# Down projections of a four-layer network on one core: seven block products in place of eight

## The reference

```python
def second_block(x, c, ...):                     # x: 512 tokens x 1024
    for l in range(DEPTH):                       # DEPTH = 2
        mod = silu(c) @ w_mod[l] + b_mod[l]
        sh1, sc1, gt1, sh2, sc2, gt2 = split(mod, 6)
        h = rms_norm(x, norm_g[l, 0]) * (1.0 + sc1) + sh1
        y = mixer_block(h, ...)                  # four mixers and w_o
        x = x + gt1 * rms_norm(y, norm_g[l, 1])
        h = rms_norm(x, norm_g[l, 2]) * (1.0 + sc2) + sh2
        y = square(relu(h @ w_up[l])) @ w_down[l]    # 1024 -> 4096 -> 1024
        x = x + gt2 * rms_norm(y, norm_g[l, 3])
    return x
```

## Time and profile before

| | |
|---|---|
| time, median of 3 runs | 1938.79 us (1936.28 to 1939.19) |
| span of the profiled execution | 1936.7 us |
| PE busy | 1863.5 us, 96% |
| DVE busy | 1182.6 us, 61% |
| ACT busy | 812.3 us, 42% |
| POOL busy | 79.3 us, 4% |
| chain of waits that ended last | PE 79%, DVE 13%, ACT 3%, issue 2% |
| granted TensorE clock, mean | 0.991 |

### The profile page before, as it was taken

The page is one execution under the profiler, slowest core; times in us unless marked ns, Lnnn a source line. Parts: engine busy times, 40 slices in busy tenths (PEclk is TensorE's granted clock), DMA queues, the critical chain, the costliest instruction groups (busy, mean ns, idle before and its releaser), DMA issues.

```text
span 1936.7 us, 25888 instructions
## 1 busy us (share of the span) xinstructions
PE 1863.5 (96%) x9834; PEld 1476.1 (76%) x9834; DVE 1182.6 (61%) x1991; ACT 812.3 (42%) x1362; POOL 79.3 (4%) x78
## 2 busy tenths in 40 slices
PE   6999998999999999999999999999999999999997
PEld 3777566887566777777988888887777898888886
DVE  5897668886698887656843234335754684323435
ACT  4554543343323345466633234224455654223322
POOL 0002100000201121000000000000000000000000
PEclk9999999999999999999999999999999999999999
DMA  9566035885001553111212222322211212222232
GB/s 368 192 224 239 1 126 204 309 329 209 8 9 39 183 186 109 66 66 66 87 49 105 90 105 87 109 88 104 92 66 44 88 66 80 94 102 93 87 109 87
DMA packets 45533, 230.72 MB, mean 119 GB/s; under 512 B 5017, under 2 KB 7066, under 8 KB 27004
## 3 DMA queue, kind: packets, MB, share of 16 engines
q1 hardware_dynamic: 45436, 229.41, 33.2%
HBM read 227.16 MB, written 2.10 MB: 118 GB/s over the span
## 4 chain that ended last, share of the span: by engine, by line
PE 79%; DVE 13%; ACT 3%; issue 2%; DMA 1%; SPq 0%; POOL 0%; DVEq 0%; ACTq 0%
PE banks L2274 15%; PE banks L2275 15%; PE banks L2276 15%; PE banks L2644 3%; PE banks L2646 3%; PE banks L2645 3%; PE banks L2538 3%; PE banks L2558 2%; PE banks L2459 2%; DVE mod_raw L1410 1%; PE banks L2673 1%; PE banks L2685 1%; PE banks L2699 1%; PE banks L2472 1%; DVE w_low L1395 1%
## 5 line engine op out<-in xcount | busy, mean ns | idle before, releaser
L2274 PE MATMUL banks<-h_high,w_high 128*128 128x512 f32 x888 | 350.0, 394 | 11.4 <-DVE w_low L1395 7.9
L1395 DVE TENSOR_TENSOR w_low<-w_raw,w_high 128x1024 fp32r<-128x1024 f32 x180 | 219.8, 1221 | 230.7 <-ACT w_high L573 230.3
L2275 PE MATMUL banks<-h_low,w_high 128*128 128x512 f32 x888 | 346.6, 390 | 0.0
L2276 PE MATMUL banks<-h_high,w_low 128*128 128x512 f32 x888 | 346.6, 390 | 0.0
L573 ACT ACTIVATE w_high<-w_raw 128x1024 fp32r<-128x1024 f32 x180 | 189.7, 1054 | 151.8 <-PE banks L2276 123.8
L2274 PEld LDWEIGHTS banks<-h_high,w_high 128*128 128x128 f32 x888 | 167.4, 188 | 53.2 <-DVE w_low L1395 12.6
L2276 PEld LDWEIGHTS banks<-h_high,w_low 128*128 128x128 f32 x888 | 167.3, 188 | 35.2
L2275 PEld LDWEIGHTS banks<-h_low,w_high 128*128 128x128 f32 x888 | 167.5, 189 | 34.8 <-issue 0.7
L2276 PE MATMUL banks<-hidden_high,w_low 128*128 128x512 f32 x480 | 186.8, 389 | 0.0
L2275 PE MATMUL banks<-hidden_low,w_high 128*128 128x512 f32 x480 | 186.7, 389 | 0.0
L2274 PE MATMUL banks<-hidden_high,w_high 128*128 128x512 f32 x480 | 186.7, 389 | 0.0
(11 more groups left out here) (543 smaller groups left out, 3459.3 us busy)
## 6 DMA issues: line engine op xcount, KB each, us to landing
w_raw<-in_wt SPq DMA_DIRECT2D x129, 1024.0 KB, 5.0
mod_raw<-in_wmod SPq DMA_DIRECT2D x128, 512.0 KB, 5.1
mod_first<-in_wmod SPq DMA_DIRECT2D x8, 1024.0 KB, 11.5
cmp_w<-in_cmp_w SPq DMA_DIRECT2D x4, 1024.0 KB, 6.9
x<-in_xT SPq DMA_DIRECT2D x2, 1024.0 KB, 7.2
dft<-in_dft SPq DMA_DIRECT2D x2, 1024.0 KB, 8.1
out_x<-x SPq DMA_DIRECT2D x8, 256.0 KB, 2.1
hy_w<-in_hy_w SPq DMA_DIRECT2D x8, 192.0 KB, 3.2
```

Of the source, the lines that this page charges most:

```text
L1395: v.tensor_tensor(low[:, :, :].rearrange("p k c -> p (k c)"), RAW[b // 2][:, b % 2, :], high[:, :, :].rearrange("p k c -> p (k c)").bitcas ...
L2274: mm(out, high[:, k, :], H[:, kk, :], start=start and k == order[0], stop=False)
L2275: mm(out, high[:, k, :], L[:, kk, :], start=False, stop=False)
L2276: last = mm(out, low[:, k, :], H[:, kk, :], start=False, stop=stop and k == order[-1])
```

## The change

The down product is done in four chunks of 1024 hidden features. After each chunk's up tiles (eight; they are no longer followed by a separate round) its product is a 2x2 block product: rows in two halves of 256 tokens, hidden features in two halves of 512, output features in two halves of 512. Eight block products become seven in Winograd's form of Strassen's scheme, with sums and differences of the blocks as operands. A block product is 2 (groups of 128 tokens) x 4 (groups of 128 hidden features) x 3 = 24 matmuls of 128x512. The activations now stand still in the array and the weights move, so y comes out token-major, 128 tokens on the partitions, and is turned by 32 transposes per layer at the end.

PE runs a chunk's seven products as eight steps w = 0 to 7 and a last product. Steps 0 to 3 add the four hidden groups of three products (named by i: 0 into bank A, 1 into E, 2 into D), steps 4 to 7 those of three others (banks A, F, D); each step is 18 matmuls. The seventh product, of 24 matmuls, comes last. Operands of weights stand in two sets, used in turn. What a step needs: one or three column sums of raw weight blocks (POOL), high parts (ACT), low parts (DVE). Between them DVE folds finished banks into the sums of y. The sums of rows of the hidden activations, with their high and low parts, are made by ACT and DVE beside the up tiles.

Core of the diff (functions of PE, POOL, DVE and ACT in this order):

```diff
             for c in range(CHUNKS):
+                for b in range(PER_CHUNK if c else 0):
+                    ...
+                    tile(Q + 8 + 2 * c + b // 4, b % 4, Hh, Hl).then_inc(w_used, 1)
+                for w in range(8):
+                    p, s, late = w % PK, w % 2, w >= PK
+                    for i in ((2, 0, 1) if w in (0, 2, 3, 4, 5, 6) else (0, 2, 1) if w == 7 else (0, 1, 2)):
+                        pe.wait_ge(*when(f"mix_l.{c}.{w}.{2 if late else 'last'}" if i == 2 else f"mix_l.{c}.{w}.0"))
+                        ...
+                        for j in range(2):
+                            if w == PK and i in (0, 2):
+                                pe.wait_ge(*when(f"y2_r.{c}.d{j}" if i == 2 else f"y2_k.0.{j}" if c == 0 else f"y2_r.{c}.a{j}"))
+                            ...
+                            product(out, (high, low), (OPh[s][:, i, :], OPl[s][:, i, :]), start, p == PK - 1).then_inc(*did(f"mix_p.{c}.{w}.{i}.{j}"))
+                for j in range(2):
+                    pe.wait_ge(*when(f"y2_r.{c}.u{j}"))
+                    ...
+                        last = product(bank(BANK_A + j), (S3h[:, p, t], S3l[:, p, t]), (T3h[p][:, :], T3l[p][:, :]), p == 0, p == PK - 1)
+                    last.then_inc(*did(f"mix_v.{c}.{j}"))
-            for n in range(14):
-                tile(Q + 20 + n // 4, n % 4, HIDh, HIDl, even=n % 2 == 0, hidden=1 if n < 2 else None).then_inc(w_used, 1)
...
+            def col_sum(c, w):
+                pool.wait_ge(*when(f"blocks{RAW_OF[w]}.{c}.{w}"))
+                if w >= 2:
+                    pool.wait_ge(*when(f"mix_p.{c}.{w - 2}.2.1"))
+                ...
+                gp.tensor_tensor(OPf[w % 2][:, 2, :], raw[:, 2, :], raw[:, 0, :], sub).then_inc(*did(f"mix_s.{c}.{w}.0"))
+            def late_sums(c, w):
+                ...
+                gp.tensor_tensor(t3[:, :], raw[:, 3, :], raw[:, 2, :], sub).then_inc(*did(f"mix_s.{c}.{w}.0"))
+                pool.wait_ge(*when(f"mix_s.{c}.{w}.0"))
+                pool.wait_ge(*when(f"mix_p.{c}.{w - 2}.0.1"))
+                gp.tensor_tensor(out[:, 0, :], t3[:, :], raw[:, 0, :], add).then_inc(*did(f"mix_s.{c}.{w}.1"))
+                pool.wait_ge(*when(f"mix_s.{c}.{w}.1"))
+                pool.wait_ge(*when(f"mix_p.{c}.{w - 2}.1.1"))
+                gp.tensor_tensor(out[:, 1, :], raw[:, 1, :], out[:, 0, :], sub).then_inc(*did(f"mix_s.{c}.{w}.2"))
...
+            def blocks_low(c, w):
+                dve.wait_ge(*when(f"mix_h.{c}.{w}.0"))
+                v.tensor_tensor(flat(OPl[w % 2], 0, 2), flat(BLOCKS[RAW_OF[w]], 0, 2), flat(OPh[w % 2], 0, 2).bitcast(f32), sub).then_inc(*did(f"mix_l.{c}.{w}.0"))
+            def late_low(c, w):
+                dve.wait_ge(*when(f"mix_h.{c}.{w}.0"))
+                v.tensor_tensor(OPl[w % 2][:, 2, :], BLOCKS[RAW_OF[w]][:, 3, :], OPh[w % 2][:, 2, :].bitcast(f32), sub).then_inc(*did(f"mix_l.{c}.{w}.2"))
+                dve.wait_ge(*when(f"mix_h.{c}.{w}.2"))
+                v.tensor_tensor(flat(OPl[w % 2], 0, 2), flat(OPf[w % 2], 0, 2), flat(OPh[w % 2], 0, 2).bitcast(f32), sub).then_inc(*did(f"mix_l.{c}.{w}.0"))
+                v.tensor_tensor(T3l[w % PK][:, :], T3f[w % PK][:, :], T3h[w % PK][:, :].bitcast(f32), sub).then_inc(*did(f"mix_l.{c}.{w}.last"))
+            def fifth_sum(c, j):
+                gather(c, "d", j, YT[:, j::2, 1, :], twice(BANK_D + j), f"mix_p.{c}.3.2.{j}", ...)
+            for c in range(CHUNKS):
+                ...
+                for w in range(2, PK):
+                    blocks_low(c, w)
+                    sum_low(c, w)
+                for w in range(PK, 8):
+                    late_low(c, w)
+                    if w == 4:
+                        for j in range(2):
+                            fifth_sum(c, j)
+                        for j in range(2):
+                            first_sum(c, j)
+                    if w == 6:
+                        for j in range(2):
+                            second_sum(c, j)
...
+            def late_high(c, w):
+                act.wait_ge(*when(f"blocks{RAW_OF[w]}.{c}.{w}"))
+                act.wait_ge(*when(f"mix_p.{c}.{w - 2}.2.1"))
+                nc.scalar.activation(OPh[w % 2][:, 2, :], BLOCKS[RAW_OF[w]][:, 3, :], ACT.Copy).then_inc(*did(f"mix_h.{c}.{w}.0"))
+                act.wait_ge(*when(f"mix_s.{c}.{w}.0"))
+                nc.scalar.activation(T3h[w % PK][:, :], T3f[w % PK][:, :], ACT.Copy).then_inc(*did(f"mix_h.{c}.{w}.1"))
+                act.wait_ge(*when(f"mix_s.{c}.{w}.2"))
+                nc.scalar.activation(flat(OPh[w % 2], 0, 2), flat(OPf[w % 2], 0, 2), ACT.Copy).then_inc(*did(f"mix_h.{c}.{w}.2"))
```

More of the change, by code:

```diff
@@ L565, in _ @@
+            if lay + 1 < LAYERS:
+                sp.wait_ge(*when(f"mix_l.{CHUNKS - 1}.6.last"))
+                load_pair(first + PER_LAYER // 4, 0)
+        for m in range(NT):
+            sp.wait_ge(*when(f"y2_x.{m}"))
+            sp.dma_start(A["out"][:, m * P:(m + 1) * P].rearrange("(k p) t -> p k t", p=P), XT[:, :, m * P:(m + 1) * P]).then_inc(*did(f"stored.{m}", 16))
+        sp.wait_ge(*when(f"stored.{NT - 1}"))
     @block.scalar
@@ new lines, in totals @@
+            def totals(j):
+                one, six = SUM1[j], SUM6[j][:, :]
+                pool.wait_ge(*when(f"y2_r.{CHUNKS - 2}.v{j}"))
+                gp.tensor_tensor(six, six, one, add).then_inc(*did(f"y2_p.{j}"))
+                gp.tensor_tensor(YT[:, j, 0, :], YT[:, j, 0, :], one, add).then_inc(*did(f"y2_q.{j}"))
+                pool.wait_ge(*when(f"y2_p.{j}"))
+                gp.tensor_tensor(YT[:, j, 1, :], YT[:, j, 1, :], six, add).then_inc(*did(f"y2_c.{j}"))
+                for h in range(2):
+                    gp.tensor_tensor(YT[:, 2 + j, h, :], YT[:, 2 + j, h, :], six, add).then_inc(*did(f"y2_d.{j}.{h}"))
@@ L1387, in _ @@
+            for m in range(2):
+                pool.wait_ge(*when(f"y2_t.{m}"))
+                gp.tensor_tensor(XT[:, :, m * P:(m + 1) * P], XT[:, :, m * P:(m + 1) * P], YF[:, m, :, :], add).then_inc(*did(f"y2_x.{m}"))
     @block.vector
@@ L1836, in _ @@
                 dve.wait_ge(*when("nf_x.7@0"))
-                dve.wait_ge(*when("y2_x.7", back="layers"))
+                for m in range(NT):
+                    dve.wait_ge(*when(f"y2_x.{m}@{lay - 1}"))
             v.tensor_copy(LM[:, :], MODV[:, ds(lay * 48 + 32, 48)]).then_inc(*did("layer_cols.mod"))
@@ new lines, in final_sum @@
+            def final_sum(m):
+                dve.wait_ge(*when(f"y2_t.{m}"))
+                v.tensor_tensor(XT[:, :, m * P:(m + 1) * P], XT[:, :, m * P:(m + 1) * P], YF[:, m, :, :], add).then_inc(*did(f"y2_x.{m}"))
+            scaled(0)
+            scaled(1)
+            seventh_sum(CHUNKS - 1, 1)
+            scaled(2)
+            gained(0)
+            gained(1)
+            scaled(3)
+            gained(2)
+            final_sum(2)
+            gained(3)
+            final_sum(3)
+            if lay + 1 < LAYERS:
+                up_low(CHUNKS, 0)
@@ L2632, in _ @@
             if lay:
+                pe.wait_ge(*when(f"y2_t.1@{lay - 1}"))
                 keep_busy(bank(1, P), 16)
-                sums("h1", 5, S)
+                for m in range(NT):
+                    pe.wait_ge(*when(f"h1_sq.{m}"))
+                    for k in range(KT):
+                        last = mm(bank(5)[:, m * P:(m + 1) * P], ONES, WIDE_SQ[m % 2][:, k * P:(k + 1) * P], start=k == 0, stop=k == KT - 1)
+                    last.then_inc(*did(f"h1_ss.{m if m < 3 else 7}"))
             first_body(Q, "h1_hi", "h1_lo", "h1")
@@ new lines, in _ @@
+            for m in range(NT):
+                pe.wait_ge(*when(f"y2_n.{m}"))
+                if m < 3:
+                    pe.wait_ge(*when(f"y2_r.{CHUNKS - 1}.{('e1', 'f1', 'g1')[m]}"))
+                else:
+                    pe.wait_ge(*when("y2_t.1"))
+                for k in range(KT):
+                    last = nc.tensor.transpose(PS[:, TURNED_AT[m] * S + k * P:TURNED_AT[m] * S + (k + 1) * P], YT[:, m, :, :].rearrange("p h c -> p (h c)")[:, k * P:(k + 1) * P], IDENT)
+                last.then_inc(*did(f"y2_mm.{m}"))
```

533 lines of the change are left out of this document (349 added, 184 removed).

## The result

| | before | changed |
|---|---|---|
| median of the runs, us | 1938.84 (1936.28 to 1939.19, 4 runs) | 1972.03 (1971.51 to 1974.43, 4 runs) |
| profiled execution, span, us | 1936.7 | 1969.7 |
| mean granted TensorE clock | 0.991 | 0.977 |
| first feed-forward part, us | 338.4 | 350.2 |

What follows compares the result with a forecast made beforehand. PE's matmuls were taken to bound the kernel, with DVE-POOL sharing deciding the change: 1936.7 - 46.6 + 65.2 + 3.6 + 2.5 + 3.0 = 1964.4 us of span, 1966 as median; forecast 1950 to 1978, 8-in-10 range 1940 to 1992.

Steps and rivals of the forecast that it cites:

- The matmuls: Down product on PE: 672 matmuls a layer, 152.3 us instead of 175.6, so 23.3 us less per layer.
- The sharing: Late steps: two-SBUF-input operations of DVE and POOL exclude each other, 5.8 us per step against 4.08 on PE.
- no sharing: Rival: POOL's and DVE's late-step work runs side by side, 16 us of stalls in all, 1911 us; chance 0.10.
- The stalls: PE waiting in the down product's chunks: 7.4 us per chunk plus 3.0, 32.6 us a layer, 65.2 for two.
- hand-overs: Passing work between engines in a chunk's chain: about 0.03 us each, some 15 per chunk, 3.6 us for eight chunks.
- 60 to 65 us ahead of L3196: Trace sign: total PE idle time ahead of these matmuls, some 4 us at step 4 and 2 at step 7.
- the walk: Timeline of a middle chunk with one shared resource: step 4 stalls 4.4 us, the whole chunk 7.4 us.
- The first chunks: Each layer's first chunk: 1.5 us added because DVE's early sums of rows meet POOL's column sums at steps 0 to 2.
- DMA: Weight loads in the down product: asked for one to two steps ahead, costed at nothing.
- The layer ends: Work behind each layer's last product: +2.5 us at the first layer's end, +3 us at the last.

Runs made afterwards that it cites:

- two_fills: Changed kernel with each of POOL's column sums replaced by two constant fills that read nothing (outputs constant, timing only): 1924.9 us, ratio 0.9931 to the kernel before.
- short_fill_fold: Changed kernel with one constant fill per POOL sum, and DVE's fifth-bank fold moved behind step 4's first low part: 1903.7 us, ratio 0.9819 to before.
- reordered: Changed kernel with two late sums moved from POOL to DVE, and the orders of DVE, POOL and TensorE rearranged: 1930.6 us, ratio 0.9959 to before.

## Why the prediction was right

**The matmuls.** 23.3 us a layer were put down. With the operands in time the part shrank from 338.4 to 315.4: 23.0 (from start to start 22.6). Right.

**The sharing.** Put down as the deciding term, with "no sharing" at 1911. By the estimate above the kernel without it would take 1929 to 1935 us, so that sharing costs 37 to 43 us. Without it the change would be faster than before, by 3 to 9 us: the sign hung on it, as argued, but on less than the 27 us that the rival had. That rival is too low by 14 us even against two_fills, whose sums are shorter. Its stalls were about right: 8 us a layer, and the second part of two_fills has 7.9 (from start to start, against short_fill_fold). The first part has 13.0: there the granted clock fell behind the stall (0.67 at 1104.3 to 1108.3), and step 4 lasts 6.18 us in three chunks where the second part has 4.6. That makes some 5 us, and the ends of the layers, longer than I had them (below), another 5.

**The stalls.** 32.6 us and 1.8 of hand-overs a layer, 34.4, were forecast; 350.2 - 315.1 = 35.1 were measured. Where I looked for idle time I was wrong in kind: 60 to 65 us ahead of L3196 were named, and the row has 45.4. (The same sentence had 4 us at step 4 and 2 at step 7, which is 48 for eight chunks; the walk itself had 7.4.) The remainder is for the most part matmuls at the low clock.

From start to start the walk holds for middle chunks: step 3 lasts 7.9 to 8.1 us in place of 4.08, 4.0 more where 4.4 were forecast, and steps 4 to 6 together last 15.2 to 16.0 in place of 12.2, where 3.0 more were forecast. In all a middle chunk is 7.3 to 8.4 us late, with 7.4 forecast. The first chunks are later than forecast, 10.2 and 11.3 us where 8.9 were put (7.4 and 1.5 for DVE's early sums of rows). Of this, 5.4 us stand at steps 2 and 3 already, where only the 1.5 had been put; step 4 then waits 2.8 us in place of 4.4. So their sum came out nearer than its parts, which is luck.

**DMA.** Put down as nothing; short_fill_fold shows a part without stalls with the same loads. In the order of reordered a load did come late, by 1.45 us in one chunk, because its wait hung on an operation that I had moved.

**The layer ends.** Start to start, the first end grew from 17.3 us to 23.5, by 6.2 where 2.5 was forecast; the last from 12.9 to 16.4, by 3.5 where 3.0 was.

```profile
1317.41 0.39 PE L3198 MATMUL banks<-col_diff_high,row_diff_low 128*128 128x512 f32 x1
...
1321.40 5.13 POOL L1562 TENSOR_TENSOR x<-x,y_features 128x1024 f32<-128x1024 f32 x2 [5.69 <-DVE y_features L2514]
1322.37 1.93 DVE L2509 TENSOR_SCALAR y_tokens<-y_tokens,stats 128x1024 f32<-128x1024 f32 x1
...
1325.99 4.68 PE L2557 MATMUL banks<-eye 128*128 128x128 f32 x32
1330.51 7.31 PE L2914 MATMUL banks<-square_wide,eye 128*128 128x128 f32 x64
1332.55 1.06 ACT L975 ACTIVATE square_wide<-x 128x1024 f32<-128x1024 f32 x1 [3.99 <-PE banks L2914]
...
1340.89 0.47 PE L2567 MATMUL banks<-h_high,w_high 128*128 128x512 f32 x1 [0.39 <-ACT h_high L680]
```

The walk ended with DVE's last addition. Behind it stand the squares: ACT has two buffers for them and waits 3.99 us for PE to sum the first, and only then comes the third. PE is late with this sum because ahead of it in its queue stand the 32 products of L2557 (`keep_busy`, whose result nothing reads), 4.68 us of them, while the first squares had been ready at 1324.9. This term was mis-sized by 3.7 us. That these are its cause is read from the trace and was not tried.

**The account.** From start to start in the two profiles: the stretch ahead of the first part -1.5, the parts +12.2 and +11.9, the first end +6.2, the second layer up to its part +0.7, the last end +3.5: 33.0 us, the difference of the spans (1969.7 - 1936.7).
